# Attention heads in pairs on both halves of the array, and a first stage that starts on x without its norm

## What is computed

```python
# first block
h = h + 0.5 * rmsnorm(swiglu(rmsnorm(h, gn[0]), ffn_w_in[0], ffn_w_out[0]), gn[1])   # first stage
h = h + rmsnorm(mlstm_mixer(rmsnorm(h, gn[2]), ...), gn[3])
h = h + 0.5 * rmsnorm(swiglu(rmsnorm(h, gn[4]), ffn_w_in[1], ffn_w_out[1]), gn[5])
# second block, twice
h = rms_norm(x, pre_norm_g[l]) * (1.0 + scale) + shift      # scale, shift, gate from c @ w_ada
proj = h @ w_in[l]                                          # q, k, v, g_att and four convolution parts
att = dilated_attention(q, k, v, rel_bias) * silu(g_att)    # 8 heads of 64
cnv = b_gate * short_conv(c_gate * u, conv_w[l]) * silu(g_conv)
x = x + gate * rms_norm(concat(att, cnv) @ w_out[l], post_norm_g[l])
def swiglu(x, w_in, w_out):                                 # 1024 -> 2 x 2816 -> 1024
    gu = x @ w_in
    return (silu(gu[..., :2816]) * gu[..., 2816:]) @ w_out
def rmsnorm(x, g):
    return x * rsqrt(mean(x * x) + 1e-6) * g
```

## Time and profile before

| | |
|---|---|
| median of three runs | 875.49 us (874.79 to 877.78) |
| profiled execution, its own time | 877.0 us |
| span of its trace | 875.0 us |
| PE busy | 849.8 us, 97% |
| DVE busy | 585.3 us, 67% |
| ACT busy | 416.5 us, 48% |
| POOL busy | 112.7 us, 13% |
| mean granted clock of TensorE | 0.988 |

### The profile page before, as it was taken

The page is one execution under the profiler, slowest core; times in us unless marked ns, Lnnn a source line. Parts: engine busy times, 40 slices in busy tenths (PEclk is TensorE's granted clock), DMA queues, the critical chain, the costliest instruction groups (busy, mean ns, idle before and its releaser), DMA issues.

```text
span 875.0 us, 15692 instructions
## 1 busy us (share of the span) xinstructions
PE 849.8 (97%) x6467; PEld 801.4 (92%) x6467; DVE 585.3 (67%) x904; ACT 416.5 (48%) x710; POOL 112.7 (13%) x133
## 2 busy tenths in 40 slices
PE   5999999999999999999999999999999999999996
PEld 5999999999899877989999999989988998888896
DVE  5777776676788555688777768775666468466533
ACT  4644444444276533445444444445645355445532
POOL 2000000121200000020000003220132302022413
PEclk9999999999999999899999999999999999999999
DMA  8777777565166422338787875517343552743421
GB/s 320 278 254 257 251 261 268 190 184 176 36 221 185 140 73 65 127 122 322 278 290 272 281 242 179 183 49 248 137 144 101 166 167 63 229 145 104 138 73 49
DMA packets 45767, 159.02 MB, mean 182 GB/s; under 512 B 5072, under 2 KB 7632, under 8 KB 45696
## 3 DMA queue, kind: packets, MB, share of 16 engines
q1 hardware_dynamic: 45696, 158.03, 54.0%
HBM read 156.94 MB, written 1.06 MB: 181 GB/s over the span
## 4 chain that ended last, share of the span: by engine, by line
PE 91%; DVE 6%; POOL 1%; ACT 1%; issue 1%; DMA 0%; SPq 0%; DVEq 0%; POOLq 0%
PE ps L114 77%; PE ps L116 14%; DVE u L116 2%; DVE tmp L116 2%; DVE yg L116 1%; POOL rst L116 1%; POOL sqa L116 0%; DVE hT L116 0%; DMA hT<-xT 0%; DVE rows L116 0%; ACT sq L116 0%; DVE w L116 0%; ACT w L116 0%; DVE sst L116 0%; ACT u L116 0%
## 5 line engine op out<-in xcount | busy, mean ns | idle before, releaser
L114 PE MATMUL ps<-u,w 128*128 128x256 f32 (+1 forms) x3887 | 503.8, 286 | 4.3 <-ACT u L116 1.1
L114 PEld LDWEIGHTS ps<-u,w 128*128 128x128 f32 x3887 | 484.2, 189 | 16.7 <-DVE u L116 7.2
L116 DVE TENSOR_TENSOR w<-raw,w 128x1024 fp32r<-128x1024 f32 x245 | 298.8, 1228 | 176.5 <-ACT w L116 175.7
L116 ACT CAST w<-raw 128x1024 fp32r<-128x1024 f32 x245 | 254.3, 1049 | 123.4 <-PE ps L116 118.1
L114 PE MATMUL ps<-h,w 128*128 128x272 f32 (+1 forms) x1000 | 129.6, 285 | 0.0
L114 PEld LDWEIGHTS ps<-h,w 128*128 128x128 f32 x1000 | 125.8, 188 | 0.0
L116 POOL TENSOR_TENSOR sqa<-sqa,sq 128x256 f32<-128x256 f32 (+1 forms) x22 | 21.5, 975 | 369.1 <-ACT sq L116 368.5
L116 DVE SCALAR_TENSOR_TENSOR acc<-adr,cact,acc 128x1024 f32<-128x1024 f32 x42 | 55.7, 1327 | 0.0
L116 ACT ACTIVATE si<-ps 128x272 f32<-128x272 f32 (+1 forms) x44 | 17.1, 392 | 73.3 <-PE ps L116 72.1
L116 PE MATMUL ps<-u,w 128*128 128x256 f32 (+1 forms) x169 | 46.7, 285 | 0.0
L114 PE MATMUL ps<-m,w 128*128 128x256 f32 x368 | 46.6, 281 | 0.0
(11 more groups left out here) (159 smaller groups left out, 721.4 us busy)
## 6 DMA issues: line engine op xcount, KB each, us to landing
raw<-wst SPq DMA_DIRECT2D x245, 512.0 KB, 4.5
adr<-wada SPq DMA_DIRECT2D x48, 512.0 KB, 3.9
Bt<-bias_rows SPq DMA_DIRECT2D x8, 192.0 KB
hT<-xT SPq DMA_DIRECT2D x4, 272.0 KB, 3.7
outT<-hT SPq DMA_DIRECT2D x2, 384.0 KB, 2.6
outT<-hT SPq DMA_DIRECT2D x1, 256.0 KB, 2.6
cs<-cst SPq DMA_DIRECT2D x1, 168.0 KB, 7.3
cs<-cst SPq DMA_DIRECT2D x1, 128.0 KB, 4.9
```

Source lines behind the costliest of these rows:

```text
L114: fn()
L116: fn().then_inc(m[0], m[1])
```

## The change

Three things change.

**First stage.** The 8 tiles of x are multiplied by the gain only and split (`first_input`), and the first block starts on them. The squares are summed meanwhile; `first_sums` stands on PE behind the second block and `first_spread` behind the third. The factor r = rsqrt(mean square + eps) is kept in `r0`; each gate block is multiplied by it on DVE ahead of Silu (`z`), while the up blocks stay without it. So `h` lacks the factor 1/r, and the norm behind the down projection makes up for it with `eps0` = eps · (mean square + eps) in place of eps. `head` isn't used here, and 12 matmuls on `dz` (`dense`) stand in front. The loads of x and of the first chunks are issued in another order. The `ada_step` of every third j moves into the first four tiles of the down projection.

**Attention.** Heads go in pairs, one pair every fourth block. `scores(k)` does both heads, one on partitions 0 to 63 into bank 4 and one on 64 to 127 into bank 7, in turn; `values(k)` does both in turn into the two halves of bank 6. The buffers `Sb` and `st_` are doubled.

**Mix.** The written order of the k tiles changes its last two.

```diff
-        for q in range(4):
-            m_x += 2 * [sp.dma(... hT[:, 2 * q:2 * q + 2, :] ...)]
-        m_cst = sp.dma(... cs[:, 0:C_MASK] ...)
+        load_x(0)
+        load_x(1)
+        load()
+        load_x(2)
+        load_x(3)
+        load()
+        m_cst = sp.dma(partial(nc.sync.dma_start, cs[:, 0:C_MASK], cst[:, 0:C_MASK]), (s_in[0], 16))
+        load()
...
+        def first_input(k):
+            g = vc[:, V_NG + k:V_NG + k + 1]
+            um1[k] = act(partial(nc.scalar.mul, u1[:, k, :], hT[:, k, :], g), m_x[k], m_vec)
+            um[k] = dve(partial(nc.vector.scalar_tensor_tensor, u2[:, k, :], hT[:, k, :], g,
+                                u1[:, k, :].bitcast(F32), ALU.mult, ALU.subtract), um1[k], m_x[k], m_vec)
...
+        for k in range(1, 4):
+            first_input(k)
+        for k in range(4):
+            first_square(k)
+        advance(0)
+        for k in range(4, KT):
+            first_input(k)
+        advance(1)
+        for k in range(4, KT):
+            first_square(k)
...
-            head(x1, x2, n, um1, um, nb=2 if n == T else HB)
+            if n == T:
+                dense(12)
+            else:
+                head(x1, x2, n, um1, um)
             for j in range(NF):
-                if j:
+                if j and (n == S or j % 3):
                     ada_step(acc)
...
+                if n == T:
+                    if j == 0:
+                        pe.wait(m_cst)
+                        first_sums()
+                        early.append(block(x1, x2, n))
+                        first_spread()
+                    z = free[bg] = dve(partial(nc.vector.tensor_tensor, zg[:, i, :], ps[:, bg, 0:n], r0, ALU.mult),
+                                       mg, first["r"], sir[i])
+                    s = sir[i] = act(partial(nc.scalar.activation, si[:, i, :], zg[:, i, :], ACT.Silu), z, hfr[i])
...
             def evac(j, b, mk):
-                if j < 3:
+                while j < 4 and 0 < ad["use"] % 24 < ((17, 20, 22, 24) if n == T else (22, 23, 24, 24))[j]:
                     ada_step(acc)
...
-        r = sums_of(T, 0, hm)
-        advance(1)
-        dve.wait(m_vec)
-        normalise(T, 0, vg(0), None, r, hm)
...
-            def scores(h):
+            def scores(k):
+                pe.wait(free[4], free[7], qm[k], qm[4 + k])
                 for t in range(2):
-                    ms = pe(partial(nc.tensor.matmul, 
-                        ps[:, 4, S * t:S * t + S], qk[hp:hp + 64, hb, 128 * t:128 * t + 128],
-                        qk[hp:hp + 64, 4 + hb, :], start=True, stop=True))
+                    for e in range(2):
+                        hp, b = 64 * e, 4 + 3 * e
+                        ms = pe(partial(nc.tensor.matmul, ps[:, b, S * t:S * t + S],
+                                        qk[hp:hp + 64, k, 128 * t:128 * t + 128], qk[hp:hp + 64, 4 + k, :],
+                                        start=True, stop=True))
...
+            def values(k):
+                pe.wait(ptm[2 * k], ptm[2 * k + 1], mV, free[6])
                 for j in range(2):
-                    mo = pe(partial(nc.tensor.matmul, ps[hp:hp + 64, 6, 0:S], Vt[:, j, 64 * h:64 * h + 64],
-                                                         PT[:, i, j, :], start=j == 0, stop=j == 1))
+                    for e in range(2):
+                        h, hp = 2 * k + e, 64 * e
+                        mo = pe(partial(nc.tensor.matmul, ps[hp:hp + 64, 6, 0:S], Vt[:, j, 64 * h:64 * h + 64],
+                                        PT[:, e, j, :], start=j == 0, stop=j == 1, skip_group_check=True))
...
+                k, part = at_ // 4, at_ % 4
+                if part == 0 and k < 4:
+                    scores(k)
+                if part == 2 and k < 4:
+                    weights2(k)
+                if part in (0, 1) and 0 < k < 5:
+                    transposes(2 * k - 2 + part)
+                if part == 3 and 0 < k:
+                    values(k - 1)
...
-                         (mx1, mx, (0, 1, 2, 4, 5, 6, 7, 3)), l == 0)
+                         (mx1, mx, (0, 1, 2, 4, 5, 6, 3, 7)), l == 0)
```

More of the change, by code:

```diff
@@ L595, in low @@
             um[k] = m
[L597 to L620, removed]
@@ L623, in build, with first_square @@
-        for _ in range(3):
-            load()
+        first, r0 = {}, tmp[:, 2, :]
+        def first_input(k):
[3 more added lines that the diff above has]
+                                u1[:, k, :].bitcast(F32), ALU.mult, ALU.subtract), um1[k], m_x[k], m_vec)
+        first_pooled = 5
+        def first_square(k):
+            i = k % 4
+            if k == 0:
+                first["acc"] = act(partial(nc.scalar.activation, sqa[:, 0, :], hT[:, 0, :], ACT.Square), m_x[0])
+                return
+            q = act(partial(nc.scalar.activation, sq[:, i, :], hT[:, k, :], ACT.Square), m_x[k], sqr[i])
+            if k < first_pooled:
+                sqr[i] = first["acc"] = pool(partial(nc.gpsimd.tensor_tensor, sqa[:, 0, :], sqa[:, 0, :],
+                                                     sq[:, i, :], ALU.add), q, first["acc"])
+            elif k == first_pooled:
+                first["sq"] = q
+            else:
+                p = (k - 1) % 4
+                first["sq"] = sqr[p] = dve(partial(nc.vector.tensor_tensor, sq[:, i, :], sq[:, p, :], sq[:, i, :],
+                                                   ALU.add), q, first["sq"])
@@ new lines, in first_sums @@
+        def first_sums():
+            i = (KT - 1) % 4
+            state["early"] = column_sums(7, sqa[:, 0, :], T, W_ONE, SUM_Y, True, False, first["acc"], m_wts)
+            m = sqr[i] = column_sums(7, sq[:, i, :], T, W_ONE, SUM_Y, False, True, first["sq"])
+            m = dve(partial(nc.vector.tensor_scalar, sst[:, 0:2], ps[:, 7, 0:4:2], EPS, None, ALU.add), m)
+            m = dve(partial(nc.vector.tensor_scalar, sst[0:16, 2:3], ps[0:16, 7, 4:5], EPS, None, ALU.add))
+            free[7] = m
+            dve.wait(m)
+            dve(partial(nc.vector.tensor_copy, msh[:, 0:3], sst[:, 0:3]))
+            dve(partial(nc.vector.tensor_scalar, eps0[:, 0:3], sst[:, 0:3], EPS, None, ALU.mult))
+            first["pow"] = state["pow"] = pool(partial(nc.gpsimd.tensor_tensor, rst[:, 0:3], sst[:, 0:3],
+                                                       eps3[:, 0:3], ALU.pow), m, m_eps)
@@ L1110, in transposes, with weights2 @@
+            def weights2(k):
+                for h in (2 * k, 2 * k + 1):
+                    i = h % 4
+                    r_ = dve(partial(nc.vector.reciprocal, st_[:, i, 4:6], st_[:, i, 2:4]), ex[h])
+                    for t in range(2):
+                        nrm[h] = pool(partial(nc.gpsimd.tensor_scalar, Sb[:, i, t, :], Sb[:, i, t, :],
+                                              st_[:, i, 4 + t:5 + t], None, ALU.mult), r_)
             def transposes(h):
-                i = h % 2
+                i = h % 4
@@ L1152, in layer @@
             wr = None
-            first = [2 * h for h in range(NH)]
             for at_ in range(21):
-                if at_ - 6 in first:
-                    values(first.index(at_ - 6))
-                if at_ - 4 in first:
-                    transposes(first.index(at_ - 4))
-                if at_ - 2 in first:
-                    weights2(first.index(at_ - 2))
-                if at_ in first:
-                    scores(first.index(at_))
+                k, part = at_ // 4, at_ % 4
[7 more added lines that the diff above has]
+                    values(k - 1)
                 while todo:
```

106 lines of the change are left out of this document (53 added, 53 removed).

## The result

| | before | after |
|---|---|---|
| median of five runs | 877.19 us | 862.55 us (859.87 to 863.47) |
| span of the profiled execution | 875.0 us | 861.3 us |
| ratio to before | | 0.9837, 95% interval 0.9814 to 0.9861 |

The three runs of the kernel before that stand above are among its five here. The changed kernel is 1.6% faster, by 14.6 us between medians and by 13.7 us between the profiled spans. The sum had been 20.6 us, so about two thirds of it came, and the parts are further from the forecast than the total.

What follows compares the result with a forecast made beforehand. PE was taken as the bound, busy 97% of the span. Start 5.1, heads without overlap 5.2 and overlap 10.3 made 20.6 us off 877.0: 856.4, less 1.5 for the median, so 855 us; range 850 to 866.5.

Steps and rivals of the forecast that it cites:

- Start: First stage up to the fifth block: begins at 24.5 instead of 30.38, 5.9 us saved, 5.1 after the clock allowance.
- `r0` 2 us later, 3: Start: if r0 comes 2 us later than worked out, only 3 us are saved.
- The clock term: Start: block 0 at the lower clock takes 1.5 us more; half of that was taken.
- Heads without overlap: Attention pairs: fewer entries and exits of scores and values save 0.65 us per pair, 5.2 us for 8 pairs.
- With overlap: Scores and values groups: neighbouring passes of different heads share slots, five of eight, saving 10.3 us.
- complete overlap: Rival for scores and values groups: four slots instead of eight, 3.4 us more saved, 851 to 852 us; chance 0.04.
- The new wait: Rival in the pair: transposes wait for POOL's four scalings, 1 us per pair, 8 in all, 863 us; chance 0.03.
- POOL's term: Attention pair: weights2 gives POOL four scalings, 3.7 us, with cover of 2 us or more before PE needs them.
- The last step: Whole kernel: the median of runs is 1.5 us below the profiled execution, so 856.4 becomes 855.
- Slower: Rival in the groups: each turn between halves empties the array, up to 0.27 us per turn, 878 to 879 us; chance 0.04.
- no overlap: Rival in the groups: passes of two halves run one behind another, 865 us; chance 0.22.
- one kind only: Rival in the groups: only scores overlap, since values share one bank, 5.2 us less saved, 860 us; chance 0.13.

Runs made afterwards that it cites:

- e1: The kernel before with the new first stage alone, heads and mix order as before: 873.77 us, ratio 0.9961.
- e9: The changed kernel with both heads' scores taken from the first head's partitions (0 to 63), banks and order unchanged: 868.59 us, ratio 0.9904.
- e4: The changed kernel with the first head's products all ahead of the second's, in scores and values, instead of in turn: 862.39 us, ratio 0.9834.
- e3: The changed kernel with the first head's transposes recorded ahead of the next pair's scores instead of behind them: 857.83 us, ratio 0.9773.
- e6: The changed kernel with the copy of r0 and the first z and hf ahead of chunk 6 on DVE: 863.03 us, ratio 0.9846.
- e2: The kernel before with heads in pairs and the new mix order, first stage as before: 864.10 us, ratio 0.9856.

## Why the prediction was right, and where it was off

**The bound** held: PE was the end's bound, and what it lost in work or in early idle time came out in the time: the start's 3.15 us and the layers' 10.9 are 14.0 of the 13.7 measured.

**Start: mechanism right, size off.** Forecast 5.1 (bounds 4.4 to 5.9, and 3 with `r0` 2 us late), measured 3.15. Both paths that were to meet at 24.5 came late: PE's own four blocks were done at 27.1 instead of 24.4, and `z` ended at 27.08. Three durations were short. Chunk 0 was there at 7.95 and not at 6.3: the 1.18 MB up to its end had to be moved, but 1.88 MB had been when it landed, so loads issued behind it were served with it. ACT was free for it at 7.6, so this cost less than it looks. DVE's split of it took 1.69 us instead of 1.2. And chunk 6 landed at 23.95 where I had 21, by the argument that the same bytes had been moved by then before. The bytes were nearly right, but the order was not kept: the 7.0 MB up to chunk 6 had been moved at 22.1, and 7.76 MB when it landed. Behind it four more chunks had been issued by 20.05, where before the queue ran empty at 21. The case "r0 2 us later, 3" gave the right number, though not `r0` alone was late. The clock term (half of 1.5) was worth all of 2.0 in the profiled run and nothing in e1.

**Heads without overlap: agrees, not taken apart.** 0.65 per pair rested on fewer entries and exits. No run shows the 5.2 by itself. e9 confirms the piece it can: its scores group, eight passes on one half, takes 1.92 where I had 8 · 0.215 + 0.2 = 1.92.

**With overlap: the step failed on the other side.** I took five slots of eight, "only neighbours from different heads can share a slot", since instructions run in program order. The runs show four of eight for both kinds, the rival "complete overlap" with a chance of 0.04, worth 6.9 + 6.9 = 13.8 instead of 10.3. e4 shows that program order isn't what decides: with the heads one after the other nothing changes. Two windows cut out of a scores group of the changed kernel show it pass by pass:

```profile
624.23 0.49 PE L116 MATMUL ps<-qk 64*128 64x256 f32 x2
```

```profile
624.23 0.70 PE L116 MATMUL ps<-qk 64*128 64x256 f32 x4
```

Within the first 0.1 us two passes have started, within 0.4 us four. They start in twos, one on each half as e9 lets conclude. The Trainium skill's rule ("TensorE: Matmul & The Clock Gate", part 3) that matmuls in different row groups start next to each other agrees with this trace. Its sentence that matmuls are strictly in program order, which I had turned into five slots, does not fit e4, where the measurement decides. The rule of "TensorEngine Tiling (Array Packing)" in the Trainium skill (Restrictions and Gotchas) on one PSUM bank doesn't reach the values: their two halves write bank 6 together and take 1.02 us. Whether it holds for the scores, which are row tiles, no run shows, since they always went to two banks.

**The new wait: place right, resource wrong.** The rival looked at `transposes` and at POOL's scalings (cover 2 us), priced at 8 us, chance 0.03. The wait came there, at the second transposes, six times, and each cost 1.31 us (the transposes could have started 0.12 behind the block's last matmul, at 628.63, and started at 629.94), 7.9 in all. What is late is bank 5: its copy `PT` stands in ACT's queue behind the next pair's exponentials. I had named what is queued behind DVE's and POOL's waits, not what `scores` queues on ACT ahead of the copy. e3 shows it. That this rival's 863 lies so close to the measured time is chance. POOL's term was also too short: 3.7 us for the four scalings, 5.57 measured for the first pair; with the copy's wait gone and the transposes a group earlier, e3 shows 0.72 us of waiting for it.

So the heads were to give 15.5: they gave 5.2 + 13.8 − 7.9 = 11.1 by the pieces and 10.9 by the windows. By these pieces the forecast's 20.6 becomes 20.6 − 2.0 + 3.5 − 7.9 = 14.2. The median came out inside the range because the start and the copy took away more than the overlap gave; that three misses of different sign stayed within it is in part luck. The last step, from 856.4 to 855, rested on a median of three runs; with five the median before is 877.19, and the 1.5 us are gone.

**Slower, no overlap, one kind only**: none happened. Turns between the halves cost nothing at all: a group of eight passes in two halves is as long as one of four.

## What to carry to other kernels

In this kernel small fp32 products with a contraction or an output of 64 doubled their pace when two heads' products stood in one group on different halves of the array, whichever order they stood in. When a stage is paired up, look through every engine's queue for what the pair puts ahead of an older result: here one copy, four instructions too late, gave back 40% of what the heads gained (7.9 of 19.0 us), and moving two lines returned most of it. A value that everything waits for (here `r0`) should stand ahead of work that waits for a load of its own.

## What the runs showed of the chip beyond that

**Two halves, two queues.** TensorE started passes of the second half ahead of passes of the first that stand earlier in the program (e4: eight passes in 1.07 us, two at a time from the start); no row of the kernel before could tell.

**POOL beside DVE.** The scaling `Sb<-Sb,st`, the same instruction, took 926 ns before and 1356 ns in the changed kernel (means of 32). Both lines are from the pages, the kernel before first:

```profile
L116 POOL TENSOR_SCALAR Sb<-Sb,st 128x256 f32<-128x256 f32 x32 | 29.3, 926 | 112.8 <-PE ps L116 72.9
L116 POOL TENSOR_SCALAR Sb<-Sb,st 128x256 f32<-128x256 f32 x32 | 42.9, 1356 | 113.8 <-DVE st L116 113.8
```

The trace shows which ones are slow. In the changed kernel's first pair the four took 1.81, 1.98, 0.92 and 0.92 us. The first two ran beside DVE's splits of chunks (TENSOR_TENSOR, from 620.91 and 622.85), the last two beside its SCALAR_TENSOR_TENSOR. In the kernel before they ran beside SCALAR_TENSOR_TENSOR and TENSOR_REDUCE and took 0.93. So a scaling took twice as long beside a split; that the two share something follows from this only as a guess, since no run took it apart.

**The granted clock at the start** depends on the execution. It can be told only by distances here: the clock column reads 1.00 for the window 10.78 to 15.77 of the changed kernel, although the matmuls of block 0 start 0.23 us apart there at first (1.2 GHz) and 0.12 at the end (2.4 GHz). With 12 filling matmuls block 0's first 23 took 4.37 to 5.03 us in six profiled runs and 3.17 and 3.18 in two (e3, e1); with 24 they took 3.06, 3.29, 3.33 and 3.06 in all four. The 12 filling matmuls all ran at the lower level (2.93 us in each of these runs) and ended 1.1 to 2.4 us ahead of block 0, and the length of this gap didn't decide: it was 2.03 us in e3, whose block was fast, and 1.13 in e6, whose block was slow. With 24 the clock rose within the filling, which took 4.7 to 5.3 us up to block 0, where 24 at 0.24 each would have taken 5.8.

**The same code, 2.35 us apart.** The kernel before and e2 are identical up to the first scores, which came at 613.73 and 611.38. At 337.8 us the two are level within 0.1, and from 389 on e2 is 2.35 ahead. The windows of 340 to 400 us show what differs: the granted clock, 0.94 in the kernel before and 0.97 in e2.

```profile
340.00:400.00 60.00, 57.67 (x421) 52.63 (x420) 45.63 (x88) 28.24 (x52) 5.84 (x8) 0.94 0.38 132
```

```profile
340.00:400.00 60.00, 58.26 (x440) 54.06 (x439) 47.96 (x92) 29.33 (x53) 5.81 (x8) 0.97 0.42 140
```

From 215 to 232 us it is the other way round, 0.90 before and 0.80 in e2. So behind norms and in the mixer's sparse stretches the granted clock is lower in different places from one execution to the next. From the fifth block to the first scores the fourteen profiled executions took 581.0 to 585.9 us. That spread is larger than the gain of the start, 3.15 us, and so the intervals there overlap. No run took the clock's share in it apart.
